# Hybrid decoder layer on one core: a shorter chain into the first expert, and the last expert's rows kept on chip for the final sum

## The reference

```python
h = jax.nn.silu(xblk @ w_gate[e]) * (xblk @ w_up[e])
return h @ w_down[e]
...
y = jnp.zeros((N, D), x.dtype).at[tok_sorted].add(yb[dest] * gate_sorted[:, None].astype(x.dtype))
```

## Time and profile before

| what | value |
|---|---|
| median of 3 runs | 2147.21 us (2146.64 to 2147.99) |
| the profiled execution | 2145.4 us, span from first to last instruction 2143.6 us |
| TensorE busy | 2062.6 us, 96% of the span |
| VectorE, ScalarE, GpSimd busy | 1269.0 us, 925.2 us, 514.2 us |
| DMA in the experts' slices | 381 to 406 GB/s |

### The profile page before, as it was taken

The page is one execution under the profiler, slowest core; times in us unless marked ns, Lnnn a source line. Parts: engine busy times, 40 slices in busy tenths (PEclk is TensorE's granted clock), DMA queues, the critical chain, the costliest instruction groups (busy, mean ns, idle before and its releaser), DMA issues. The chain is left out here.

```text
span 2143.6 us, 36559 instructions
## 1 busy us (share of the span) xinstructions
PE 2062.6 (96%) x14742; PEld 1673.5 (78%) x14743; DVE 1269.0 (59%) x1291; ACT 925.2 (43%) x1069; POOL 514.2 (24%) x377
## 2 busy tenths in 40 slices
PE   8998999999999999999999999999899999999996
PEld 6777777767787887888887788788688888888882
DVE  4767422234410565356478723356788888888885
ACT  4672122242101553022246421001677777777763
POOL 4232311112340102233323332201122222222100
PEclk9999999999999999999999999999899999999998
DMA  4445544424431544321143422231799999999986
GB/s 151 134 123 195 181 118 124 128 99 161 160 132 37 128 109 154 113 69 40 50 133 119 175 86 99 101 118 59 265 406 389 389 382 388 385 381 386 384 332 240
DMA packets 138137, 408.48 MB, mean 191 GB/s; under 512 B 38736, under 2 KB 60112, under 8 KB 112800
## 3 DMA queue, kind: packets, MB, share of 16 engines
q1 hardware_dynamic: 123104, 367.40, 48.8%
q10 hardware_dynamic: 5552, 22.02, 2.7%
q0 software_dynamic: 9360, 17.32, 2.2%
HBM read 353.53 MB, written 69.93 MB: 198 GB/s over the span
## 5 line engine op out<-in xcount | busy, mean ns | idle before, releaser
L3612 DVE TENSOR_TENSOR ex_sb_low<-landed,high 128x2048 fp32r<-128x2048 f32 x192 | 431.0, 2286 | 61.4 <-ACT high L3541 57.9
L3541 ACT CAST high<-landed 128x2048 fp32r<-128x2048 f32 x186 | 346.2, 1912 | 38.4 <-PE ex_ps_u L169 35.5
L3426 POOL DMA_INDIRECT y_rows<-ex_sb_y,slot_row x32 | 32.2, 1006 | 438.7 <-ACT ex_sb_y L3556 414.5
L167 PE MATMUL ex_ps_g<-high,ex_sb_xt 128*128 128x512 f32 x260 | 104.9, 403 | 2.4 <-DVE ex_sb_xt L3606 2.4
L169 PE MATMUL ex_ps_g<-high,ex_sb_xt 128*128 128x512 f32 x260 | 102.1, 393 | 0.0
L168 PE MATMUL ex_ps_g<-ex_sb_low,ex_sb_xt 128*128 128x512 f32 x260 | 102.0, 392 | 0.0
L167 PE MATMUL ex_ps_u<-high,ex_sb_xt 128*128 128x512 f32 x260 | 101.4, 390 | 0.5 <-DVE ex_sb_low L3612 0.5
L169 PE MATMUL ex_ps_u<-high,ex_sb_xt 128*128 128x512 f32 x260 | 101.2, 389 | 0.0
L168 PE MATMUL ex_ps_u<-ex_sb_low,ex_sb_xt 128*128 128x512 f32 x260 | 101.2, 389 | 0.0
L169 PE MATMUL ex_ps_y<-high,ex_sb_ht 128*128 128x512 f32 x248 | 96.8, 390 | 0.0
L167 PE MATMUL ex_ps_y<-high,ex_sb_ht 128*128 128x512 f32 x248 | 96.6, 390 | 0.0
(11 more groups left out here) (704 smaller groups left out, 5575.2 us busy)
## 6 DMA issues: line engine op xcount, KB each, us to landing
landed<-exp_up SPq DMA_DIRECT2D x64, 1024.0 KB, 8.3
landed<-exp_gate SPq DMA_DIRECT2D x64, 1024.0 KB, 7.7
landed<-exp_down SPq DMA_DIRECT2D x62, 1024.0 KB, 8.5
chunk_ch<-slab SPq DMA_DIRECT2D x4, 2048.0 KB, 7.5
merged_d<-room SPq DMA_DIRECT2D x16, 512.0 KB, 2.9
landed<-ssm_c SPq DMA_DIRECT2D x16, 512.0 KB, 4.8
cb_sb_y<-y_rows SPq DMA_DIRECT2D x16, 512.0 KB, 9.5
si_sb_w<-w_tiles SPq DMA_DIRECT2D x14, 512.0 KB, 3.6
```

The source lines that it names most:

```text
L167: nc.tensor.matmul(out, lhs[0], rhs[0], start=start, stop=False)
L3426: pool.indirect_dma_start(k.y_rows, bass.IndirectOffsetOnAxis(ap=k.slot_row[:, e:e + 1], axis=0), y[e % 2][:, :], None, bounds_check=2 * T ...
L3541: nc.scalar.copy(part_half(high[part], h), part_half(k.landed[part], h)).then_inc(high_ready[part], 1)
L3612: nc.vector.tensor_tensor(part_half(low[part], half), part_half(k.landed[part], half), part_half(high[part], half), ALU.subtract).then_inc ...
```

## The change

1. out_project: 5 idle products for 14. VectorE builds at_place for the first choice in one operation (768 wide); GpSimd builds the six of the second only, after both ranks.
2. route: the product by the identity goes behind the counts; the two idle products are gone.
3. experts, the first one: x is turned in two halves with semaphores of their own, copied and cut by halves; six idle products stand before the first gate product, whose second half of channels waits for the second half of x.
4. experts, the last one: its y is not scattered. GpSimd clears the rows of y_rows that it would have written (a scatter of zeros, at e = 4). The choice weights are computed before the body of expert 29 and after it. GpSimd writes them to share_d, one element at a time, and gathers each row's own, before it comes to the scatter of expert 28. ScalarE and VectorE write the last expert's rows, times their weight, as high and low part into last_y. VectorE builds at_token, a 0/1 matrix of row against token (1024 wide). The overflow lists are made before times_up(31).
5. The loads of y_rows move from combine into the experts block of SyncE, behind the wait for the scatter of expert 30. They land in the buffers of high and low weight parts.
6. overflow_experts: TensorE runs three idle products in the branch that is taken.
7. combine: for each half of a tile two products more, at_token with last_y (float32r). PSUM for four tiles ahead instead of two. ScalarE runs a root on one element first, which brings its table. No idle products. The scaling goes into a buffer of its own (g) and comes right after the mean, before the result of the tile before; the last tile is joined and stored by halves.

```diff
-        picks, IDLE_PRODUCTS = s.sem("picks"), 14
+        picks, IDLE_PRODUCTS = s.sem("picks"), 5
...
+                pool.wait_ge(rank_ready, 4)
+                for n in range(EARLY):
+                    nc.gpsimd.tensor_scalar(at_place[:, 1, n, :], iota[:, :], rank[:, 1, n:n + 1], None, ALU.is_equal
+                                            ).then_inc(placed, 1)
...
+                v.tensor_tensor(at_place[:, 0], iota[:, :].unsqueeze(1).to_broadcast([P, EARLY, P]),
+                                rank[:, 0].unsqueeze(2).to_broadcast([P, EARLY, P]), ALU.is_equal).then_inc(first_placed, 1)
...
+                for b in range(2):
+                    sp.wait_ge(y_out[b], ROWS_OUT[b])
+                sp.wait_ge(rows_cleared, 16)
+                for part, read in ((1, E + 1), (2, E)):
+                    sp.wait_ge(used[part], read)
+                    for t in range((part - 1) * NT // 2, part * NT // 2):
+                        load_rows(sp, k, t, k.y_in[t])
...
+                    if e == 4:
+                        pool.wait_ge(cleared, 2)
+                        pool.indirect_dma_start(k.y_rows, bass.IndirectOffsetOnAxis(ap=k.slot_row[:, E - 1:E], axis=0), nought, None,
+                                                bounds_check=2 * T - 1, oob_is_err=False).then_inc(rows_cleared, 16)
+                pool.wait_ge(shared, 2)
+                for n in range(2):
+                    pool.dma_start(k.share_d[n * T:(n + 1) * T].rearrange("(t p) a -> p (t a)", p=P), k.gates[:, :, n],
+                                   allow_slow_non_contiguous=True).then_inc(share_out, 16)
+                pool.wait_ge(share_out, 32)
+                pool.indirect_dma_start(share[:, :], None, k.share_d, bass.IndirectOffsetOnAxis(ap=k.slot_row[:, E - 1:E], axis=0),
+                                        bounds_check=2 * T - 1, oob_is_err=False).then_inc(share_in, 16)
+                for e in range(E - 4, E - 1):
                     scatter(e)
...
+                for n in range(IDLE_BEFORE_GATE):
+                    nc.tensor.matmul(ps_y[:, n % 2, :], high[0][:, 0:P], high[0][:, 0:HALF], start=True, stop=True)
+                for c in range(KD):
+                    if c % (KD // 2) == 0:
+                        pe.wait_ge(*((first_low, 1), (x_low_ready, 2))[c // (KD // 2)])
+                        pe.wait_ge(low_ready[0], 1 + c // (KD // 2))
+                    m = product(0, 0, 0, ps_g[:, :], xt[0], c, c * DE, KD)
...
+                act.wait_ge(share_in, 16)
+                for half, ps in enumerate((ps_g, ps_u)):
+                    act.wait_ge(last_done, half + 1)
+                    nc.scalar.activation(k.last_y[0][:, half * HALF:(half + 1) * HALF], ps[:, :], ACT.Copy, scale=share[:, :]
+                                         ).then_inc(last_high, 1)
...
+                        for n, y in enumerate(rows_of(k, t)):
+                            nc.tensor.matmul(out, diag[t % 2][n][:, :], y[:, ends[half]], start=(n == 0), stop=False)
+                        for n in range(2):
+                            m = nc.tensor.matmul(out, at_token[:, t, :], k.last_y[n][:, ends[half]], start=False, stop=(n == 1))
+                        m.then_inc((half_weighted, weighted)[half], 1)
...
-                for b in range(2):
-                    act.wait_ge(k.y_out[b], 8 * E)
+                nc.scalar.activation(warm[:, :], eps[:, :], ACT.Sqrt).then_inc(table_in, 1)
...
+                for t in range(1, LAST):
+                    join(t)
+                    scale(t)
+                    norm(t - 1)
+                join_halves(LAST, 1)
+                scale(LAST)
+                norm(LAST - 1)
```

More of the change, by code:

```diff
@@ L3337, in gather, with rows_of, load_rows @@
                             bounds_check=T - 1, oob_is_err=False).then_inc(k.x_in[b], 16)
+def rows_of(k, t):
+    half, at = t // (NT // 2), t % (NT // 2) * D
+    return [rows[half][:, at:at + D] for rows in k.rows_kept]
+def load_rows(eng, k, t, landed):
+    for n, y in enumerate(rows_of(k, t)):
+        eng.dma_start(y, k.y_rows[n * T + t * P:n * T + (t + 1) * P, :]).then_inc(landed, 16)
 def part_half(t, h):
@@ L3355, in experts @@
     with Space(nc, "ex") as s:
-        high, low = k.high, [s.sb(f"low{n}", [P, KD * DE], F32R) for n in range(3)]
+        high, low = k.high, k.low
         xb = k.xb
@@ L3430, in _ @@
                 pool.sem_inc(y_free, 2)
+                nc.gpsimd.memset(nought, 0.0).then_inc(cleared, 1)
+                nc.gpsimd.memset(share[:, :], 0.0).then_inc(cleared, 1)
                 for e in range(2, E):
@@ L3565, in _ @@
                 high_first(1)
-                high_x(0, 0)
+                for n, half in enumerate(halves):
+                    act.wait_ge(*((first_turned, 1), (x_turned, 3))[n])
+                    nc.scalar.copy(xt[0][0][:, half, :], ps_x[:, half, :]).then_inc((first_high, x_high_ready)[n], 1)
                 high_first(2)
@@ L3627, in _ @@
                 low_w(0, 0, 0)
-                low_x(0, 0)
+                for n, half in enumerate(halves):
+                    dve.wait_ge((first_high, x_high_ready)[n], 1)
+                    nc.vector.tensor_tensor(xt[0][1][:, half, :], ps_x[:, half, :], xt[0][0][:, half, :], ALU.subtract
+                                            ).then_inc((first_low, x_low_ready)[n], 1)
                 low_w(0, 0, 1)
@@ L3708, in overflow_experts, with blocks @@
             "linked", "again_set", "picked", "counted", "ranked", "listed", "slots_done", "over_listed"))
-        def blocks(eng, body, ahead=lambda: None):
+        def blocks(eng, body, ahead=lambda: None, behind=lambda: None, instead=lambda: None):
             none = eng.value_load(k.unused[0:1, 0:1], min_val=0, max_val=1)
@@ L3719, in blocks @@
                         pass
+                behind()
             with eng.Else():
-                pass
+                instead()
         with s.block() as block:
@@ L3784, in list_over, with idle @@
                     pe.wait_ge(over_listed, 2)
-                blocks(pe, body, list_over)
+                def idle():
+                    for n in range(IDLE_AHEAD):
+                        mm(ps_y[:, n % 2, :], k.high[0][:, 0:P], k.high[0][:, 0:HALF], start=True, stop=True)
+                blocks(pe, body, list_over, instead=idle)
             @block.scalar
```

225 lines of the change are left out of this document (128 added, 97 removed).

## The result

The changed kernel takes 2154.9 us (median of 7 runs) where the kernel before takes 2147.2 beside it: ratio 1.0031, 95% interval 1.0020 to 1.0042. That is 7.7 us by the medians and 6.7 by the ratio. It is inside the whole range on record (2141 to 2156), but outside the forecast's own (2145 to 2152), 6 us above its 2149 and nearest to the 2154 of rival 1. By the bound of 0.2% it is slower, to which the forecast gave 0.33. The profiled execution took 2150.1 us with a span of 2148.3; it was the fastest of the seven.

A forecast was written before the change was run, and what follows sets the result against it. TensorE was taken as the bound in the experts. Front -6.8, last experts +2.5 and end +6.0 summed to +1.7 us, median about 2149; range 2141 to 2156, the forecast's own 2145 to 2152.

The forecast's parts named there:

- rival 1: Last experts: the weights' write is slow, over 13 us, and ScalarE waits 8 us; sum +6.8, 2154; chance 0.25.
- The two late terms: The forecast's terms for the last experts, +2.5 us, and for the end, +6.0 us.
- Front: Last token tile's norm to first expert's gate products: shorter waits and a faster clock, -6.8 us (-5 to -7.5).
- Last experts: Around experts 29 to 31: GpSimd's weights write delays y_free and so ScalarE, +2.5 us (0 to 7.6).
- D: Last experts: the delay of ScalarE behind the weights' write, taken as 3 us.
- cost is D less 0.45: Last experts: VectorE's overflow arithmetic ends at 2078.1 against 2078.58 for times_up(31), so delay D costs D - 0.45.
- the nearest row: Last experts: the write priced by a scatter under full DMA, 8.3 us to landing, so the second lands near 2070.
- End: Barrier of the experts to the span's end: SyncE's loads, table load, clock and tiles, +6.0 us (+3.0 to +7.5).
- the scatter of expert 30 lands 3.4 us after 2086.26: End: it lands at 2089.7, and only then SyncE issues the 16 loads of y, until 2098.0.
- The drain behind a table load: Combine: the skill's 1.38 us on top of the 1.28 us load, left out; with it the end would be +7.4.

The follow-up runs named there:

- e2: The changed kernel with points 1 to 3 of the change taken back; ratio to the kernel before 1.0066.
- e1: The kernel before with points 1 to 3 of the change alone; ratio to the kernel before 0.9958.
- e9: The changed kernel with the weights written by one DMA from the memory of k.gates, without a new tile; ratio to the kernel before 1.0002.
- e11: The kernel before with an unused tile of 64 bytes a partition ahead of all tiles of the experts; ratio to the kernel before 1.0005.
- e3: The changed kernel with the weights in a new tile of 64 bytes a partition, written by one DMA; ratio to the kernel before 1.0059.
- e5: The changed kernel with the weights written by one DMA from a new tile of 128 bytes a partition; ratio to the kernel before 1.0047.
- e6: The kernel before with an unused tile of 64 bytes a partition behind the high weight parts; ratio to the kernel before 1.0069.
- e10: The changed kernel with one-DMA weights write without new tile, 4 early y loads, root behind first diagonals, more idle products (12 behind last down); ratio to before 0.9959.
- e12: The kernel of e10 with 7 idle products behind the last down product instead of 12; ratio to the kernel before 0.9957.

## Right and wrong, by the forecast's own steps

The time came out inside the range, but partly by luck. The two late terms missed in the same direction, 1.7 and 3.8 us, and only the width that rival 1 gave the range holds them. Its 2154 is near by luck too: it had 7.6 + 6.0 where 4.2 + 9.8 came.

*Front* (-6.8; profile -6.9): each part held against the profile that it was worked out from. The choice starts 1.9 us sooner after the norm (forecast 2.0), fold 2.2 more (2.2), silu of expert 0 another 2.7 (2.6). VectorE's 768-wide comparison took 0.96 us (0.95). What the step lacked is a range upwards: it trusted one profile for the clock of the old front. Against e2 the front is worth 8.6, and e1's runs give 9.0 (6.4 to 11.6).

*Last experts* (+2.5; +4.2): D is by how much ScalarE keeps expert 29's y too late. The rule "cost is D less 0.45" held to 0.2 us, but D was 4.87 for 3. The failing step is the choice of the nearest row, a scatter's 8.3 us to landing, for pieces of 4 bytes: the second write landed 11.0 us after its issue, and it took 12.7 from first issue to gather. Rival 1 was to decide above 13, so this was its near miss, and the mechanism on record for it is the one that worked. The Trainium skill (DMA: Bandwidth & Descriptors, Rules for kernel authors), one descriptor per element for a non-contiguous last dimension, was the better guide: e9 against the changed kernel bears it out with 5.2 against 10.8 us. By the page's fixed 2 us (Anatomy of one DMA) even the cheap write would be done sooner than it was: e9 has 5.8 us from its issue to the gather.

*End* (+6.0; +9.8): SyncE's issues took 8.35 us (8.26), it came 9.4 us after VectorE (over 5), the seven tiles took 30.3 (30.3), the tail 5.9 (5.95). The failing step is "the scatter of expert 30 lands 3.4 us after 2086.26": the loads of y started 2.9 us later, relative to the last product, than this gives. The row was read in a kernel whose DMAs had no small pieces to work off; e9 gives 2.7 of it back. By what way the pieces reach a scatter issued 17 us after they have landed is not shown. From SyncE's last issue to combine it took 4.0 us (forecast 3.2), and the first tile 0.4 more than forecast, while the first product came 0.3 sooner after combine's start. Together they make the 3.8 to within 0.2. The drain behind a table load, left out in the forecast, is absent here as well: the warm root starts at 2101.20, the load ends at 2101.19. The Trainium skill (ScalarE: Activation LUTs, What ACT_TABLE_LOAD costs) would have 1.38 us between them.

So the mechanisms were right and two sizes were off, for the most part for one cause, the 4-byte pieces. Their second effect, on another transfer, was not thought of.

*Left open*: why a move of tiles by 64 bytes makes products longer; which of the moved tiles it is was not tried.

## What to carry to other kernels

Price a DMA by its pieces, not its bytes, and count what the pieces do to every transfer behind them; 8 KB in 2048 pieces cost 6 to 7 us here, and one DMA of 64 bytes a partition cost 0.1 us. A load issued early inside a block moves that block's barrier by its issue time: move only as many as are needed first. When an experiment adds even a small tile, compare the steady pace before reading anything else.

## What the runs showed of the hardware

The place of tiles in SBUF relative to one another changed the pace of TensorE by 2 to 3%:

| moved | period, us | product (L168), mean ns |
|---|---|---|
| nothing (before, changed, e9) | 17.73 | 389 |
| all tiles by 64 bytes (e11) | 17.73 | 389 |
| x, h and y by 64 bytes against the weight parts (e3) | 18.17 | 395 |
| the same by 128 bytes (e5) | 18.10 | 394 |
| low parts, x, h and y by 64 bytes against the high parts (e6) | 18.26 | 399 |

In e3 and e5 the three products of a step of up grow alike (394 to 396 ns). In e6 the third (L169, low x with the high part) grows least, to 392, where the first two reach 398 and 399. In the kernels with the good period all these tiles lie at the same offset modulo 2048 bytes, by the program: their sizes are multiples of that and no small tile is between them. The Trainium skill (SBUF — State Buffer, SBUF: two separate sides) says that TensorE never waits for another engine's accesses; no run here shows whether the longer products are a wait for another engine or between TensorE's own two reads.

TensorE's clock was not the same in the same stretch of the same code from one profile to the next: 0.63 and 0.50 over the idle products of the routing block (before and e2). In one profile each, twelve idle products ahead of a gap of 1.8 us left it at 1.00 behind the gap (e10), and seven ahead of a gap of 3.0 us left it at 0.50 (e12).

While the 2048 pieces of 4 bytes were written, the DMA engines were 60 to 87% busy and moved 33 to 45 GB/s; in 1600 to 1700 of the kernel before they moved 389.
